# Two-block transformer forward on one core: other orders on the engines, folded norm sums, causal squares held as 384 columns

## The reference, cut to what matters

```python
a_d = softmax(q0 k0) - lam * softmax(q1 k1)      # causal, rotated q and k
o_d = rmsnorm(a_d @ v_d, subln) * (1 - lambda_init)
o_f = softmax(q k * scale + cum_i - cum_j) @ v_f # causal
x = x + concat(o_f, o_d) @ w_out
```

## Time and profile before

| | us |
|---|---|
| median of 3 runs | 1978.85 |
| profiled execution, its own time | 1984.81 |
| its span (first to last instruction) | 1982.7 |
| PE matmul busy | 1736.3 (88%) |
| PE weight load busy | 1488.5 (75%) |
| DVE busy | 849.1 (43%) |
| ACT busy | 583.5 (29%) |
| POOL busy | 174.4 (9%) |
| mean granted clock of PE | 0.919 |

### The profile page before, as it was taken

How to read it: one execution, slowest core, us unless ns; L and a number is a source line. 1 busy time by engine, 2 the same in 40 slices (tenths; PEclk the granted TensorE clock), 3 DMA queues, 4 the chain that set the end, 5 groups by cost and what they waited for, 6 DMA issues and landing times.

```text
span 1982.7 us, 34259 instructions
## 1 busy us (share of the span) xinstructions
PE 1736.3 (88%) x14366; PEld 1488.5 (75%) x14367; DVE 849.1 (43%) x1534; ACT 583.5 (29%) x869; POOL 174.4 (9%) x204
## 2 busy tenths in 40 slices
PE   8999989777676776779999888999999998889997
PEld 6888858543333443469999767999999997679996
DVE  1224142311111111166556546655665566456555
ACT  2001030210000000153334344433443344444332
POOL 1000020000000000000000221100100001311001
PEclk9898879698888888879999889999999998899998
DMA  8432103399999999925556334455445564343551
GB/s 358 180 113 96 64 32 134 130 427 426 426 426 427 425 427 425 427 112 191 192 191 223 137 119 160 153 180 183 187 164 188 191 221 162 112 174 129 192 191 54
DMA packets 40395, 433.81 MB, mean 219 GB/s; under 512 B 4475, under 2 KB 4619, under 8 KB 5348
## 3 DMA queue, kind: packets, MB, share of 16 engines
q1 hardware_dynamic: 39460, 427.49, 55.4%
q0 software_dynamic: 832, 4.81, 0.6%
HBM read 431.22 MB, written 3.16 MB: 219 GB/s over the span
## 4 chain that ended last, share of the span: by engine, by line
PE 53%; DMA 19%; DVE 8%; POOL 3%; ACT 2%; issue 2%; DVEq 0%; POOLq 0%; SPq 0%; ACTq 0%
DMA ring<-moe_w_dram 18%; PE bank L747 14%; PE bank L748 13%; PE bank L749 13%; PE bank L455 3%; POOL probs L400 2%; PE bank L711 2%; DVE lo_last L1410 1%; PE bank L889 1%; DVE probs L1712 1%; PE bank L469 1%; DMA ring<-layer_w_dram 1%; PE bank L728 1%; PE bank L909 1%; DVE lo_first L1410 1%
## 5 line engine op out<-in xcount | busy, mean ns | idle before, releaser
L747 PE MATMUL bank<-h_hi,w_hi 128*128 128x256 f32 x1792 | 511.8, 286 | 9.2 <-DVE h_lo L1402 9.2
L748 PE MATMUL bank<-h_lo,w_hi 128*128 128x256 f32 x1792 | 505.5, 282 | 0.0
L747 PEld LDWEIGHTS bank<-h_hi,w_hi 128*128 128x128 f32 x1792 | 345.0, 193 | 16.8 <-issue 15.4
L748 PEld LDWEIGHTS bank<-h_lo,w_hi 128*128 128x128 f32 x1792 | 340.0, 190 | 0.2
L749 PE MATMUL bank<-h_hi,lo_last 128*128 128x256 f32 x1088 | 307.6, 283 | 0.0
L1141 ACT CAST w_hi<-ring 128x2048 fp32r<-128x2048 f32 x120 | 228.8, 1907 | 198.0 <-DMA ring<-layer_w_dram 179.4
L1410 DVE TENSOR_TENSOR lo_last<-ring,w_hi 128x2048 fp32r<-128x2048 f32 x72 | 164.9, 2290 | 108.5 <-ACT w_hi L1141 108.5
L747 PE MATMUL bank<-hid_hi,w_hi 128*128 128x256 f32 x704 | 201.1, 286 | 9.9 <-DVE lo_last L1416 9.9
L749 PEld LDWEIGHTS bank<-h_hi,lo_last 128*128 128x128 f32 x1088 | 208.1, 191 | 0.0
L748 PE MATMUL bank<-hid_lo,w_hi 128*128 128x256 f32 x704 | 200.7, 285 | 0.0
L749 PE MATMUL bank<-h_hi,lo_first 128*128 128x256 f32 x704 | 197.6, 281 | 0.0
(11 more groups left out here) (308 smaller groups left out, 2337.9 us busy)
## 6 DMA issues: line engine op xcount, KB each, us to landing
ring<-moe_w_dram SPq DMA_DIRECT2D x128, 1536.0 KB, 25.4
ring<-layer_w_dram SPq DMA_DIRECT2D x120, 1536.0 KB, 6.5
ring<-first_w_dram SPq DMA_DIRECT2D x22, 1536.0 KB, 7.5
bias_copies_dram<-bias_rows_dram POOLq DMA_DIRECT2D x1, 2048.0 KB, 10.6
area<-bias_copies_dram POOLq DMA_DIRECT2D x1, 1536.0 KB, 11.7
x_t<-x_dram SPq DMA_DIRECT2D x1, 1024.0 KB, 5.0
out_dram<-h_t SPq DMA_DIRECT2D x1, 1024.0 KB, 3.9
consts<-consts_dram SPq DMA_DIRECT2D x1, 603.5 KB, 8.1
```

The costliest lines, as they stand in the source:

```text
L747: pe.matmul(out_ap, a_hi, b_hi, start=start, stop=False, **flags)
L748: pe.matmul(out_ap, a_hi, b_lo, start=False, stop=False, **flags)
```

## The change

- In the attentions' squares (queries on partitions) the first 128 queries keep only the first 128 keys: one head is 384 columns (`SEEN`) in place of 512. Scores, exponents, normalising, turns (three in place of four) and values use those.
- The column sums of both layer norms: DVE and POOL fold eight blocks to two, PE adds two.
- In the second layer norm `h_hi` is made by ACT from the x without bias (its product with the gain is added), `h_lo` between DVE's scalings, and `lo_a(0)` and `lo_a(1)` move from DVE to POOL (`first_lo`). An early square root on ACT stands ahead of the squares in both.
- Feed-forward: ACT does silu, `hi_a(c+2)`, `hi_b(c+1)`; DVE gate, `lo_b(c)`, hidden, `lo_a(c+2)`.
- Mixer: other orders on PE, ACT and DVE. The difference heads' mean squares are taken with tokens on partitions (eight matmuls of one column, one root and one reciprocal of 128 by 8), and spread back by eight matmuls with a broadcast factor as weights; one DVE instruction per two heads applies them.

The diff, cut to its core:

```diff
-LOCAL = T + P
+LOCAL = T
+SEEN = (slice(0, P), slice(P, 3 * P))
...
+            def front_folded(n):
+
+                pool.wait_ge(S("x_updates"), PAIRS * (n - 1) + 2)
+                pool.tensor_tensor(h_t[:, 0:2, :], x_t[:, 0:2, :], x_t[:, 2:4, :], ALU.add)\
+                    .then_inc(S("front_folded"), 1)
+
+            def first_lo(q):
+
+                pool.wait_ge(S("hi_a_ready"), q + 1)
+                pool.tensor_tensor(lo_of(q)[:, part_a], ring[:, PLACES[q], part_a], hi_of(q)[:, part_a].bitcast(F32),
+                                   ALU.subtract).then_inc(S("lo_a_ready"), 1)
 
             def scaled(layer, f):
...
+            front_folded(1)
...
+            front_folded(2)
             pool.wait_ge(S("x_updates"), 2 * PAIRS)
             pool.dma_start(three["late"], late_in).then_inc(S("late_loaded"), 16)
+            first_lo(0)
+            first_lo(1)
             for layer in range(LAYERS):
...
+            def folded_sums(n):
+
+                for bank, src in enumerate((h_t, sq)):
+                    pe.wait_ge(S("folded"), 2 * n - 1 + bank)
+                    for b in range(2):
+                        last = pe.matmul(half(bank, 0), ones, src[:, b, :], start=b == 0, stop=b == 1)
+                    last.then_inc(S("sum_ready"), 1)
...
+                def diff_sums():
+                    pe.wait_ge(S("od_sq_ready"), 2 * layer + 2)
+                    pe.wait_ge(S("rope_done"), 4 * layer + 4)
+                    for n in range(2 * 4):
+                        m = pe.matmul(ps[7][:, n:n + 1], sq[:, n // 2, n % 2 * P:(n % 2 + 1) * P], ones[:, 0:1],
+                                      start=True, stop=True)
+                    m.then_inc(S("od_sum_ready"), 1)
+
+                def diff_factors(i):
+
                     if i == 0:
+                        pe.wait_ge(S("od_recip_ready"), layer + 1)
                     else:
+                        pe.wait_ge(S("diff_made"), 2 * layer + 1)
+                    for n in range(4):
+                        m = pe.matmul(ps[7][:, n * P:(n + 1) * P],
+                                      diff_stat[:, 4 * i + n:4 * i + n + 1].to_broadcast([P, P]), ident,
+                                      start=True, stop=True)
+                    m.then_inc(S("od_factors"), 1)
...
                 rotate(0)
                 factor_per_token()
                 project(3)
-                rotate(1)
                 score(0)
                 lam_sum()
+                rotate(1)
                 project(4)
+                score(1)
                 rotate(2)
-                score(1)
                 project(5)
+                score(2)
                 turn(0)
                 rotate(3)
                 cumulated()
-                score(2)
                 project(6)
+                score(3)
+                turn(1)
                 values(0)
-                turn(1)
-                score(3)
                 project(7)
+                score(4)
+                turn(2)
                 values(1)
-                turn(2)
-                score(4)
                 project(8)
+                score(5)
+                turn(3)
                 values(2)
-                turn(3)
-                diff_sums(0)
-                score(5)
                 project(9)
+                score(6)
+                turn(4)
                 values(3)
-                turn(4)
-                score(6)
                 project(10)
+                score(7)
                 turn(5)
-                diff_sums(1)
-                score(7)
+                diff_sums()
                 project(11)
+                diff_factors(0)
+                turn(6)
                 values(4)
-                turn(6)
+                diff_factors(1)
                 values(5)
                 out_part(0)
-                out_part(1)
                 turn(7)
                 values(6)
-                out_part(2)
-                out_part(3)
+                out_part(1)
                 values(7)
-                for k in range(4, KB):
+                for k in range(2, KB):
                     out_part(k)
...
                 table_for_root()
                 hi_a(at + 2)
+                hi_b(at)
                 norm_root(value, ACT.Silu)
                 for c in range(CHUNKS):
                     n = CHUNKS * (2 * layer + f) + c
-                    if c:
-                        hi_a(at + c + 2)
                     act.wait_ge(S("gate_scaled"), n + 1)
                     sg = gated[:, n % 2, :]
                     act.activation(sg, sg, ACT.Silu).then_inc(S("silu_done"), 1)
-                    hi_b(at + c)
+                    if c:
+                        hi_a(at + c + 2)
+                    if c < CHUNKS - 1:
+                        hi_b(at + c + 1)
...
                 exponents(1)
+                hi_a(at + 8)
                 copy_turned(0)
-                hi_a(at + 8)
                 exponents(2)
+                hi_a(at + 9)
                 copy_turned(1)
...
+                hi_a(at + 13)
+                copy_turned(5)
+                exponents(7)
                 evacuate(10)
-                copy_turned(5)
-                hi_a(at + 13)
-                exponents(7)
-                diff_root(1)
+                root("od_var_ready", layer + 1, diff_stat, diff_stat, "od_std_ready")
                 a_part_used(act, at + LAYER_UNITS - 1)
+                act.wait_ge(S("diff_made"), 2 * layer + 1)
+                mixed_hi(0, 2)
+                copy_turned(6)
+                evacuate(11)
...
+            def normed_hi(k):
+
+                act.activation(h_hi[:, k, :], x_t[:, k, :], ACT.Identity, scale=norm_gain(1, k),
+                               bias=first_bias[:, k:k + 1]).then_inc(S("h_hi_ready"), 1)
+
             hi_a(0)
+            table_for_root()
             squares("centred", 2)
             hi_a(1)
-            layer_norm_tail(2, "ln2_b", "x_updates")
+            layer_norm_tail(2, "ln2_b", "x_updates", normed_hi)
             for layer in range(LAYERS):
                 swiglu(layer, 0)
...
                 dve.wait_ge(S("x_updates"), PAIRS * n)
+                own(tt(h_t[:, 2:4, :], x_t[:, 4:6, :], x_t[:, 6:8, :], ALU.add))
+                dve.wait_ge(S("front_folded"), n)
+                tt(h_t[:, 0:2, :], h_t[:, 0:2, :], h_t[:, 2:4, :], ALU.add).then_inc(S("folded"), 1)
                 dve.wait_ge(S("sum_ready"), 2 * n - 1)
                 own(ts(stat[:, 0, :], ps[0][:, 0:T], 1.0 / D, None, ALU.mult))
-                if n == 2:
-                    lo_a(0)
                 for p in range(PAIRS):
                     pair = x_t[:, 2 * p:2 * p + 2, :]
                     tt(pair, pair, over(stat[:, 0, :], 2), ALU.subtract).then_inc(S("centred"), 1)
-                if n == 2:
-                    lo_a(1)
+                dve.wait_ge(S("sq_ready"), PAIRS * (n - 1) + 2)
+                own.mark(tt(sq[:, 0:2, :], sq[:, 0:2, :], sq[:, 2:4, :], ALU.add))
+                dve.wait_ge(S("sq_ready"), PAIRS * n)
+                own(tt(sq[:, 4:6, :], sq[:, 4:6, :], sq[:, 6:8, :], ALU.add))
+                tt(sq[:, 0:2, :], sq[:, 0:2, :], sq[:, 4:6, :], ALU.add).then_inc(S("folded"), 1)
                 dve.wait_ge(S("sum_ready"), 2 * n)
...
+                    if n == 2 and k >= 2:
+                        tokens_lo(1, k - 2)
+                if n == 2:
+                    tokens_lo(1, KB - 2)
+                    tokens_lo(1, KB - 1)
...
-                    if c:
-                        lo_a(at + c + 2)
                     dve.wait_ge(S("a_used"), sum(i % LAYER_SLOTS != FFN2_AT - 1 for i in range(at + c + 1)))
                     sg, hid = gated[:, n % 2, :], hidden[:, n % 2, :]
                     tt(sg, ps[bank][:, 0:T], stat[:, 3, :], ALU.mult).then_inc(S("gate_scaled"), 1)
                     if f == 0 and c == 4:
                         layer_constants(layer)
+                    lo_b(at + c)
                     dve.wait_ge(S("silu_scaled"), n + 1)
                     own(tt(hid, sg, ps[bank][:, T:2 * T], ALU.mult))
                     own(dve.tensor_copy(hid_hi[:, n % 3, :], hid))
                     tt(hid_lo[:, n % 3, :], hid, hid_hi[:, n % 3, :].bitcast(F32), ALU.subtract)\
                         .then_inc(S("hid_made"), 1)
-                    lo_b(at + c)
+                    if c:
+                        lo_a(at + c + 2)
...
+                def diff_variance():
+                    dve.wait_ge(S("od_sum_ready"), layer + 1)
+                    ts(diff_stat, ps[7][:, 0:8], 1.0 / P, EPS, ALU.mult, ALU.add).then_inc(S("od_var_ready"), 1)
+
+                def diff_reciprocal():
+                    dve.wait_ge(S("od_std_ready"), layer + 1)
+                    dve.reciprocal(diff_stat, diff_stat).then_inc(S("od_recip_ready"), 1)
 
                 def diff_norm(i):
 
+                    dve.wait_ge(S("od_factors"), 2 * layer + i + 1)
+                    pair = slice(2 * i, 2 * i + 2)
```

(33 more changed lines are left out.)

192 lines of the change are left out of this document (85 added, 107 removed).

## The result

1898.13 us (median of 4 runs, 1896.23 to 1901.12) against 1977.96 for the kernel before, run beside it; ratio 0.9591, 95% interval 0.9562 to 0.962. The profiled execution took 1896.23 us (span 1894.1) against 1984.81, 88.6 us less; 91.7 had been forecast for it, and a median of 1887 in a range of 1868 to 1920. The kernel before, run beside each experiment too, had medians from 1977.96 to 1984.57, so small differences between experiments are read from stretches of the profiles and not from these ratios.

The account below looks back on a forecast made before the run. TensorE bounds the feed-forwards; elsewhere its waits and lowered clock cost time. Savings 66.8 + 17.6 + 4.8 + 0 + 2.5 = 91.7 us take the profiled 1984.81 to 1893.1, median 1887, range 1868 to 1920.

Parts of the forecast that it names:

- Mixers, 66.8: Both mixers, projection 3 to next feed-forward: new orders, 384 columns and difference heads save 33.8 + 33.0 = 66.8 us.
- the tenth kept back: Mixers: 3.5 us a layer held back from the ideal gain for waits a hand schedule overlooks.
- A ring: Mixers: reciprocals stand behind the next score's reading, whose score TensorE issues after the turn it waits at; 22.2 us waits.
- Feed-forward ends, 17.6: Ends of the first three feed-forwards: waits for the last chunk's `lo_b` go, 10.0 us, plus 7.6 of half clock.
- Half of which is lost time, 7.6: Feed-forward ends: half clock of 6.1, 5.8 and 3.4 us behind the waits goes too, half counted as lost, 7.6 us.
- Second layer norm, 4.8: Second layer norm: TensorE starts 6.8 us earlier, less 2.0 of centring held by GpSimd; 4.8 us, bounds 2.5 and 6.8.
- First layer norm, 0: First layer norm: folds replace mostly overlapped sums; 0 us, between 0.5 won and 2 lost.
- Attention, 2.5: First block's attention: last head's chain a quarter shorter, and 0.1 per head on VectorE; 2.5 us, bounds 1 and 4.
- Rival B: VectorE is held by GpSimd in mixers, 23 us, and layer norm, 2.5 us; time 1912, chance 0.15.
- Rival A: Mixers: turns stop waiting, but one late step per slot drops the clock; half the gain goes, 1920, chance 0.18.
- C: Feed-forward: silu waits behind `hi_a(c+2)` and `hi_b(c+1)` in each of 88 chunks; slower, 2063 us, chance 0.03.
- D: Waits only change their names, TensorE bound by another chain of the same length; about 1979 us, chance 0.02.

Follow-up runs that it names:

- dve_old: Changed kernel with VectorE's old place of the reciprocals in the mixers, TensorE and ScalarE in the new order; median 1923.30 us.
- pe_old: Changed kernel with TensorE's old order in the mixers, VectorE and ScalarE in the new order; median 1899.13 us.
- both_old: Changed kernel with both VectorE's and TensorE's old order in the mixers; median 1944.47 us.
- best: Changed kernel with first two weight subtractions on VectorE, old first layer norm sums, chunk 1's cast and subtraction ahead of silu and gate; 1888.47 us.
- ffn_old: Changed kernel with the feed-forwards' old orders on ScalarE and VectorE; median 1909.03 us.
- before_again: The kernel before the change, unedited, run and profiled once more; 1985.92 us (one run).
- cols512: Changed kernel with every head's square held as 512 columns again, in attention and mixers, all orders new; median 1912.37 us.

## Why the prediction came out so

The mechanisms were right in the main; the size, within 3.1 us of 91.7 for the profiled executions, was partly luck. The mixers gave more than forecast and the feed-forwards less, and ahead of the first feed-forward 4.9 us of scatter stood in for 4.3 that did not come. The median came out 11 us above 1887, since I took the changed kernel's profiled run to lie 6.0 us over its median, as before's did; it lay 1.9 under.

- *Mixers, 66.8: too small by 5.8.* The step that failed is the tenth kept back "for waits that a hand schedule overlooks", 3.5 us a layer. Followed the schedule had none, and there was none for a turn or a value; TensorE's work in the stretch was priced at 99.9 us and took 99.67 and 101.16, the excess being clock. The terms in it: sums 1.84 and factors 1.98 for 1.9 each; a score of the first four heads 0.86 us for 0.96, of the last four 2.10 for 2.52, 2.1 us a layer where I took 1.7. "A ring" was right, shown by dve_old, pe_old and both_old, though only the two edges together close it fully.
- *Feed-forward ends, 17.6: too large by 9.5.* The gaps are 10.1 us as priced (10.0). "Half of which is lost time, 7.6" was 5.4 (best against ffn_old 15.5 in all, less the gaps; not measured by itself). Overlooked: moving `lo_a(c+2)` behind the hidden chunk makes the third chunk's weights late, 3.3 us, and, outside the orders altogether, the operands' shift, 4.1. 10.1 + 5.4 - 3.3 - 4.1 = 8.1.
- *Second layer norm, 4.8: 1.4 by the two profiles*, and 1.6 lost against before_again, whose norm took 24.27; either is under the bound of 2.5. In the two profiles of before the length goes with the clock, 27.24 us at 0.63 and 24.27 at 0.76; in the changed kernel the clock is 0.50, and how much of the miss is the clock's was not measured:

```profile
835.21:861.06 25.85, 6.24 (x25) 3.61 (x25) 17.34 (x21) 10.50 (x15) 10.83 (x4) 0.50 0.54 227
...
841.69:868.93 27.24, 14.34 (x48) 10.65 (x49) 15.95 (x23) 12.10 (x20) 0.54 (x1) 0.63 0.52 218
...
845.82:870.09 24.27, 11.37 (x48) 8.67 (x49) 15.96 (x23) 12.24 (x20) 0.54 (x1) 0.76 0.60 253
```

Mechanism and culprit were right. The failed step is which pass is caught: not the centring for 2.0 us but the second fold of x for 4.5, since GpSimd's subtraction starts at 840.67, behind its own short fold, and not at the 847.2 that I had worked out.
- *First layer norm, 0:* right within its bounds; 0.5 longer by the two profiles, 0.3 won against best's old sums.
- *Attention, 2.5:* right. Its last value products start 4.9 us earlier, 280.26 for the earlier trace rows, but 2.8 of that is its own earlier start; over the stretch itself it is 2.1, and cols512 gives 2.3 back.
- *Rival B* had the collision right and the victim wrong in the mixers: GpSimd, on slack. *Rival A* did not come about: in layer 1 the clock fell (0.98 over the stretch), at a place with no late step. *C:* silu and casts never held a chunk. *D* is out.

## What to carry to other kernels

Where two in-order engines wait for each other, look for every edge of the ring and move them together; one edge alone may show nothing. Compare profiles by stretches between fixed events, not by the whole: behind the first feed-forward matmul they repeated to 0.02 us in the changed kernel, and a stretch whose work did not change but whose length did gave away the moved operands. Work given to GpSimd should not start just ahead of a two-input pass on VectorE's critical chain; a wait of VectorE's own is the better place. And where a chain through the engines bounds a stage, less work for TensorE can lower its clock: the attention won 2.1 us at a clock of 0.60 for 0.81.
